# Moving the turn of the residual rows and the router product from between two tiles to behind the next tile's first two scores

## The reference, cut to what matters

```python
def _layer(h, pos, attend, s0, lb, attn_norm, w_in, ...):
    hn = _rmsnorm(h, attn_norm)
    z = hn @ w_in
    cq, ckv_pre, kr_pre, hq, hf, hi, hg = jnp.split(z, ...)
    ...
    o_lat = attend(q_lat, q_rope, ckv, krope)                 # 8 heads, chunk-causal softmax
    o_mla = jnp.einsum('bshc,chv->bshv', o_lat, w_uv).reshape(B, S, MLA_WIDTH)
    o_hg, s_new = _hgrn2(hq, hf, hi, hg, lb, hg_gnorm, s0)    # 4 heads of 128
    h = h + jnp.concatenate([o_mla, o_hg], axis=-1) @ w_o     # the residual rows
    h = h + _hier_moe(_rmsnorm(h, ffn_norm), w_rg, b_rg, w_re, b_re, w1, w3, w2)
    ...

def _hier_moe(x, w_rg, b_rg, w_re, b_re, w1, w3, w2):
    t = x.reshape(-1, D)
    p_group = jax.nn.softmax((t @ w_rg).astype(jnp.float32) + b_rg, axis=-1)   # 4 groups
    e_logits = ((t @ w_re).astype(jnp.float32) + b_re).reshape(-1, 4, 4)       # 16 experts
    ...
```

## Time and profile before

| what | value |
|---|---|
| median of 3 runs | 1255.17 us (1254.02 to 1258.17) |
| profiled execution, span from first to last instruction | 1250.0 us |
| PE busy | 1103.3 us, 88% of the span |
| DVE busy | 706.6 us, 57% |
| ACT busy | 515.8 us, 41% |
| mean granted TensorE clock | 0.942 of full speed |

### The profile page before, as it was taken

How to read it: one execution, slowest core, us unless ns; L and a number is a source line. 1 busy time by engine, 2 the same in 40 slices (tenths; PEclk the granted TensorE clock), 3 DMA queues, 4 the chain that set the end, 5 groups by cost and what they waited for, 6 DMA issues and landing times.

```text
span 1250.0 us, 18370 instructions
## 1 busy us (share of the span) xinstructions
PE 1103.3 (88%) x5873; PEld 892.4 (71%) x5873; DVE 706.6 (57%) x1348; ACT 515.8 (41%) x935; POOL 356.9 (29%) x379
## 2 busy tenths in 40 slices
PE   5999999989879889999989999983899999999930
PEld 4889899965457777777777777772777777878820
DVE  4320610146656666566555564437877777777757
ACT  4333222123421221323232323321877778778813
POOL 2100500001631111111111100101565566656657
PEclk9999999998988898899999998996999999999975
DMA  7340141141777585555545453754888787867576
GB/s 276 98 157 1 51 143 43 50 121 43 254 255 293 196 279 189 182 202 179 187 155 189 149 202 127 255 196 148 286 308 308 250 275 247 293 236 262 190 243 252
DMA packets 105765, 242.84 MB, mean 194 GB/s; under 512 B 15248, under 2 KB 63840, under 8 KB 95456
## 3 DMA queue, kind: packets, MB, share of 16 engines
q0 software_dynamic: 23328, 122.17, 27.8%
q1 hardware_dynamic: 81312, 117.42, 27.5%
q10 hardware_dynamic: 1056, 2.36, 0.6%
HBM read 243.31 MB, written 48.94 MB: 234 GB/s over the span
## 4 chain that ended last, share of the span: by engine, by line
PE 61%; DMA 10%; DVE 7%; issue 7%; ACT 5%; POOL 4%; SPq 4%; POOLq 1%; ACTq 0%; DVEq 0%
DMA below<-in_w 7%; PE ps L1018 6%; PE ps L881 4%; PE ps L899 4%; PE ps L2116 4%; PE ps L2117 4%; PE ps L2118 4%; PE ps L977 3%; PE ps L1056 3%; PE ps L1057 3%; SPq L1356 3%; PE ps L1060 3%; PE ps L2111 3%; PE ps L2110 3%; PE ps L2112 3%
## 5 line engine op out<-in xcount | busy, mean ns | idle before, releaser
L1773 DVE TENSOR_TENSOR low<-below,high 128x1024 fp32r<-128x1024 f32 x128 | 156.5, 1255 | 38.8 <-ACT high L1470 37.4
L1568 PE MATMUL ps<-high 128*128 128x512 f32 x384 | 157.6, 411 | 13.3 <-DVE low L1783 6.8
L1442 POOL TENSOR_TENSOR low<-below,high 128x1024 fp32r<-128x1024 f32 x64 | 132.8, 2077 | 98.1 <-ACT high L1490 97.2
L1569 PE MATMUL ps<-low,high 128*128 128x512 f32 x384 | 152.5, 397 | 0.0
L1570 PE MATMUL ps<-high,low 128*128 128x512 f32 x384 | 152.3, 397 | 0.0
L1470 ACT ACTIVATE high<-below 128x1024 fp32r<-128x1024 f32 x128 | 130.4, 1069 | 42.7 <-DMA below<-in_w 41.8
L618 ACT ACTIVATE arena<-ps 128x512 f32<-128x512 f32 (+8 forms) x100 | 51.7, 527 | 188.7 <-PE ps L881 188.2
L881 PE MATMUL ps<-arena 128*128 128x128 f32 (+4 forms) x613 | 95.7, 280 | 9.4 <-ACT arena L861 3.4
L762 POOL DMA_DIRECT2D high<-wo_dram x34 | 18.6, 547 | 296.9 <-PE ps L1060 286.2
L1968 POOL TENSOR_SCALAR arena<-arena 128x1 f32<-128x1 f32 (+5 forms) x38 | 19.3, 507 | 270.1 <-ACT arena L839 114.5
L1568 PEld LDWEIGHTS ps<-high 128*128 128x128 f32 x384 | 73.5, 191 | 30.5 <-issue 14.9
(11 more groups left out here) (245 smaller groups left out, 2256.9 us busy)
## 6 DMA issues: line engine op xcount, KB each, us to landing
below<-in_w SPq DMA_DIRECT2D x256, 256.0 KB
high<-wo_dram POOLq DMA_DIRECT2D x36, 1024.0 KB, 5.3
low<-wo_dram POOLq DMA_DIRECT2D x36, 1024.0 KB, 8.1
below<-in_w POOLq DMA_DIRECT2D x64, 512.0 KB
y_dram<-arena SPq DMA_DIRECT2D x32, 512.0 KB
arena<-in_x_prompt SPq DMA_DIRECT2D x15, 512.0 KB
below<-in_w_in SPq DMA_DIRECT2D x14, 512.0 KB, 8.0
out<-arena SPq DMA_DIRECT2D x9, 512.0 KB, 2.6
```

Source lines behind the costliest of these rows:

```text
L1442: pool.tensor_tensor(w2_lo[s % UN][:, c], w2_in[:, c], w2_hi[s % UN][:, c].bitcast(F32), ALU.subtract).then_inc(s_w2lo, 1)
L1568: pe.matmul(out, x_hi, w_hi, start=start, stop=False)
L1569: pe.matmul(out, x_hi, w_lo, start=False, stop=False)
L1773: dve.tensor_tensor(chunk(w13_lo[j], c), chunk(w13_in, c), chunk(w13_hi[j], c).bitcast(F32), ALU.subtract).then_inc(s_w13lo, 1)
```

## The change

`hnt` and `rt` of tile i - 2 are now taken at tile i: `hnt` behind `score` 0 (and `hf`), `rt` behind `score` 1. For the tile before the last they stand behind `score` 6 and `score` 7 of the last tile. Those of the last tile stay at the end. In the queue of SP `load_fq` now goes before the load of the residual rows, which waits for the later `hnt`.

```diff
@@ -457,6 +457,10 @@
             side = ({1: "wot"} if i + 1 < NT else {1: "wot", 6: "sq", 7: "hn"}).get(hd)
             if hd == 0:
                 STEPS.append(("hf", i, 0))
+            if i >= 2 and hd < 2:
+                STEPS.append((("hnt", "rt")[hd], i - 2, 0))
+            if i + 1 == NT and hd >= 6:
+                STEPS.append((("hnt", "rt")[hd - 6], i - 1, 0))
             if i and side:
                 STEPS.append((side, i - 1, 0))
             if i and hd in WO_AT[i]:
@@ -475,8 +479,6 @@
         STEPS.append(("attn", i, 7))
         if 0 < i < NT - 1:
             STEPS.append(("hn", i - 1, 0))
-        if i:
-            STEPS.append(("hnt", i - 1, 0))
         if i + 1 < NT:
             STEPS.append(("hk", i + 1, 0))
         STEPS.append(("mpv", i, 0))
@@ -485,8 +487,6 @@
             STEPS.append(("qt", i + 1, 0))
             if i + 2 < NT:
                 STEPS.append(("hs", i + 2, 0))
-        if i:
-            STEPS.append(("rt", i - 1, 0))
     STEPS += [("wot", NT - 1, 0)] + [("wo", NT - 1, n) for n in range(WO_PARTS)]
@@ -741,12 +741,12 @@
             sp.dma_start(hn_dram[t * P:t * P + R, :], hn_row[0:R, :]).then_inc(s_hnst, 16)
+            if i + 3 < NT:
+                load_fq(i + 3)
             if i + 2 < NT:
                 sp.wait_ge(s_h1st, 16 * (i + 1))
                 sp.wait_ge(s_pt, PT_GROUP[("hnt", i, 0, 1)] + 1)
                 load_residual(i + 2)
-            if i + 3 < NT:
-                load_fq(i + 3)
```

## The result

| | before | after |
|---|---|---|
| median of the timed runs | 1254.79 us (1252.24 to 1258.17, 6 runs) | 1262.44 us (1257.21 to 1263.83, 6 runs) |
| span of the profiled execution | 1250.0 us | 1259.6 us |

The ratio is 1.0071 with a 95% interval of 1.0043 to 1.0100: 0.7% slower. Forecast were 1267.8 us, or 1.010.

A forecast was written before the change was run, and what follows sets the result against it. PE was taken to bound the kernel, busy 1103.3 of 1250.0 us. Terms 11.8 + 0 + 1 - 1 + 0.8 + 0 = +12.6 gave a span of 1262.6, plus 5.17 to the median: 1267.8 us, range 1258 to 1276.

The forecast's parts named there:

- four bands: Forecast 1263 to 1271 us (0.62), more clock stretches 1271 to 1280 (0.18), clock up 1250 to 1260 (0.12), hidden 1254 to 1258 (0.08).
- The router product: Seven seams: PE idles about 1.72 us once it leaves, and it costs full length behind score 1; +11.8 us.
- The residual turn: Seven seams: its cost behind score 0 equals the mean 0.9 us given back before the mpv turn; 0 us.
- New waits: Where moved work lands, PE comes 0.3 to 0.7 us early for copies with 256 columns; +1 us over all seams.
- covered waits: At i = 8 the first projection matmul's 0.93 us wait behind an exponential goes, as PE is later; -1.0 us.
- last tile: Work put behind scores 6 and 7 costs 2.7 us, partly given back at the end; +0.8 us.
- The sum: All terms on the profiled span of 1250.0 us: +12.6 us, a span of 1262.6 us.
- The clock: Behind meta in seven seams, stretches at 1.2 GHz stay; 0 us, from -15.4 to about +10.
- The two rows it went by: Lone router product behind the last head at full clock; seam to i = 1, idle plus meta only, clock down.
- the clock stays up: Rival: parting product and meta scores ends all seven half-clock stretches; -2.8 us, 1252.4 us; chance 0.12, wholly or in most seams.
- The clock falls more often: Rival: product behind score 1 beside a wait in narrow tiles adds three short stretches; +5 us, 1273 us; chance 0.18.
- hidden anyway: Rival: PE idle just behind the first scores would hide the product; +0.8 us, 1256 us; chance 0.08.

The follow-up runs named there:

- experiment 1: Kernel before with the router product alone moved behind score 1 of the next tile, residual turn left in the seam: 1.0094 (1265.43 us).
- experiment 2: Changed kernel plus eight unneeded 20-column matmuls (narrow filler) ahead of the meta scores in each of seven seams: 1.0083.
- experiment 4: Turns of the queries put ahead of the recurrence's output (ho): 0.9913 on the changed kernel, 0.9933 on the kernel before.
- experiment 5: Kernel before with the router product alone moved behind score 1, plus turns of the queries put ahead of ho: 0.9975.
- experiment 8: Kernel before and changed kernel, both unaltered, each profiled once more: spans of 1252.0 and 1260.5 us.
- experiment 3: Changed kernel plus unneeded 512-column matmuls (wide filler) ahead of the meta scores in seven seams: 1.0064 with three, 1.0010 with two.
- experiment 7: Changed kernel with the router product of the first eight tiles made twice in a row where it now stands: 1.0298.

## Why the prediction held, point by point

The direction, the mechanism and the place were right, and the time lies in the range of 1258 to 1276 us. It lies just below the forecast's own band (1263 to 1271) and in none of the four bands. The size was 12.6 us against 7.7 by the medians, 9.6 and 8.5 by the two pairs of profiles; the interval of the ratio is 5 to 13 us.

- *The router product.* Forecast: an idle of about 1.72 us in front of L964 in seven seams, the product paid in full, +11.8 us. Measured: 1.65 us, the wait's total up by 14.0 - 2.9 = 11.1. Experiments 1, 2 and 4 show the cause: alone it makes the loss, the gap is free, and without the wait the loss of the whole change is gone. By itself it cost 1.0094, which is 11.8 us.
- *The residual turn.* Forecast 0 us, with 1.39 us given back at i = 7 (1.41 measured). In waits it is L881 behind L861 +3.1, L881 behind its copies -1.9, together some 1 us. Right for this kernel; experiment 5 shows that the judgement doesn't carry over to one without the wait.
- *New waits, covered waits, last tile.* Forecast +1, -1, +0.8. The rows show +1.3 (L1073 and L971), -1.0 (L1056) and 0.86 us for the wait on L1254 that the product used to cover.
- *The sum.* From the last start that the change doesn't touch, the `L899` of experiment 8, to the start of the last product, PE's rows over just that stretch (before, then after), with the same number of records:

```profile
408.31:843.95 435.64, 407.39 (x2442) 0.95 0.55 193
```

```profile
407.85:852.90 445.05, 405.03 (x2442) 0.96 0.54 189
```

  It is 9.4 us longer: PE's idle goes from 435.64 - 407.39 = 28.3 to 40.0 us, +11.8, its busy time by -2.4, of which some 1.7 us go with 3.4 us less at half clock. In the second pair it is 10.9 us longer, idle +12.1. So the idle rose nearly as the sum of 12.6 had it. Why PE's busy time falls by another microsecond is not shown.
- *The spans and the median.* They differ from these 9.4 and 10.9 us by what isn't the change: the changed kernel came to the stretch 0.46 and 1.13 us earlier, and took 0.65 us more and 1.3 us less behind it, which gives 9.6 and 8.5. The 5.17 us that the forecast put between span and median were not all outside the instructions: every run that lists its span took 1.8 to 2.0 us more than it. By that the first profile of before was an execution of some 1252 us, about 3 us faster than the median, while that of the changed kernel was 1 us faster than its own; this is where 9.6 against 7.7 comes from.
- *The clock.* Forecast: seven stretches at half clock behind `meta`, nothing saved. The sum held: 34.1 us in both profiles, and 0.9453 against 0.9445 to 0.9452 over all runs. The places did not: in each profile of the changed kernel six of the seven seams have one (i = 3 is without in the first, i = 2 in the second), and two and five more stand some microseconds ahead of a seam. The forecast's 30.7 us had left out one of that kind, at 515 us. The two rows it went by also change from one execution to the next, so that it came out at zero is partly luck. In the second profile of before the clock falls during the lone product (0.66 over 827 to 832 us), and behind the `meta` of i = 1 it does not fall in the first profile after, with the same idle of 1.65 us.
- *The rival "the clock stays up"* fell for the changed kernel, and its condition was named wrongly. It was not enough to part product and meta scores; the idle has to go as well. Where wide work or `ho` stands in its place (experiments 3 and 4), the clock does stay up in most seams; wide instead of narrow filler is worth 9 us.
- *"The clock falls more often"* and *"hidden anyway"* did not happen; experiment 7 shows the first for twice the product. A remark in the first was wrong, that work bound by weight loads doesn't get slower at half clock: see the last section.

The rule of the Trainium skill ("TensorE: Matmul & The Clock Gate", Part 1: the gate opens with activity, closes after idling) led to the right expectation, that the change gains nothing by the clock. Its reading as idleness fails on the seams of before, where PE's matmul records stand back to back and the clock falls, and on the narrow filler, which removes the idle and leaves 37.5 us at half clock, while the wide filler leaves 23.9.

## What to carry to other kernels

In this kernel work on the engine that sets the end was free where it stood beside a wait for another engine; before moving it, look for the row that would start next and for what releases it, and price the move by the change in the waits. If the gap is to go, take away the wait: here the copy had only to be asked for 2.7 us earlier. And the filler of the gap bears on the clock too: here wide work was a better filler than narrow. Compare the granted clock of all runs and not only of the profiled one: single profiles of the same kernel differed by 3.4 us at half clock between 419 and 820 us.

## What the runs showed of the hardware that was not expected

- Two useless float32 matmuls of 512 columns in each of seven gaps (0.87 us apiece) made the kernel 0.6% faster, 1.0010 against 1.0071, with a mean granted clock of 0.9546 against 0.9453.
- Matmuls of 16 or 20 columns behind 128-column weight loads keep PE busy (1.00 in the windows) and still let the clock fall. 3.6 us of them in a row, product and meta scores, did so at each of six seams in both profiles of before; at i = 2, the seventh, the short product, 0.56 us of idle and the meta scores did. It is no certainty: with the narrow filler it was six of seven, with the doubled product four of seven. 1.8 us of them between wide ones did so at one of fourteen seams (experiment 3).
- Such matmuls get slower at 1.2 GHz by nearly a factor of two. The last product in the first and in the second profile of before, and the second's clock over it (PE alone):

```profile
843.95 1.93 PE L1073 MATMUL ps<-arena 128*128 128x20 f32 x16 [0.78 <-ACT arena L618]
```

```profile
844.77 3.35 PE L1073 MATMUL ps<-arena 128*128 128x20 f32 x16 [0.78 <-ACT arena L618]
...
845.00:850.00 5.00, 3.13 (x16) 0.50 0.26 107
```

  From 845.0 us on, its last 14 matmuls start within 2.7 us, so 0.21 us apart, where the same product at 1.00 has 0.114 us.
